# Output projection of both layers: token tiles taken in pairs, seven half-size products for eight

## The reference, cut to what matters

```
for layer in range(DEPTH):                     # DEPTH = 2
    h = rms_norm(x, norm_g[layer])
    cols = split_columns(h @ w_in[layer])
    ... y_gdn, y_mla, y_rwkv
    mix = jnp.concatenate([y_gdn, y_mla, y_rwkv], axis=-1)
    mix = mix * jax.nn.silu(cols['gate'])
    x = x + mix @ w_out[layer]                 # (1024 x 1024) @ (1024 x 1024), float32
return rms_norm(x, final_norm_g)               # then the second block
```

## Time and profile before

| | us |
|---|---|
| median of 3 runs | 3735.61 (3733.98 to 3739.67) |
| span of the profiled execution | 3728.9 |
| stage `out0`, first transpose to last VectorE write | 1028.55 to 1160.73 |
| stage `out1`, the same | 2153.04 to 2301.77 |
| TensorE busy in the span | 3471.1 (93%) |
| VectorE busy | 2265.8 (61%) |
| ScalarE busy | 1230.6 (33%) |

### The profile page before, as it was taken

The page is one execution under the profiler, slowest core; times in us unless marked ns, Lnnn a source line. Parts: engine busy times, 40 slices in busy tenths (PEclk is TensorE's granted clock), DMA queues, the critical chain, the costliest instruction groups (busy, mean ns, idle before and its releaser), DMA issues. The chain is left out here.

```text
span 3728.9 us, 65858 instructions
## 1 busy us (share of the span) xinstructions
PE 3471.1 (93%) x27928; PEld 2115.2 (57%) x27928; DVE 2265.8 (61%) x4019; ACT 1230.6 (33%) x2149; POOL 285.3 (8%) x233
## 2 busy tenths in 40 slices
PE   7888989989999889988999988999999997999999
PEld 4367446666644467445676644666666664444444
DVE  3586468876653477458976653567766667433453
ACT  3353354535432254354534532122212221321002
POOL 0010100000000011100000000222222220000000
PEclk9999999999999999999999999999999998999999
DMA  4334112220053333312220042111111102213221
GB/s 164 105 92 129 63 40 85 81 101 12 10 190 117 98 93 100 95 40 85 79 104 12 9 157 82 35 45 42 46 41 46 41 23 89 87 41 112 90 96 45
DMA packets 302164, 281.51 MB, mean 75 GB/s; under 512 B 18208, under 2 KB 274592, under 8 KB 301872
## 3 DMA queue, kind: packets, MB, share of 16 engines
q1 hardware_dynamic: 301872, 277.30, 23.1%
HBM read 203.93 MB, written 73.33 MB: 74 GB/s over the span
## 5 line engine op out<-in xcount | busy, mean ns | idle before, releaser
L3528 DVE SCALAR_TENSOR_TENSOR cv<-glu,params,cv 128x1024 f32<-128x1024 f32 x240 | 361.0, 1504 | 6.4
L1542 PE MATMUL ps<-hT,w_cols 128*128 128x512 f32 x576 | 254.6, 601 | 8.3 <-PEq L160 8.3
L413 PE MATMUL ps<-hT,w_cols 128*128 128x512 f32 x448 | 196.0, 595 | 1.6 <-PEq L160 1.6
L1542 PEld LDWEIGHTS ps<-hT,w_cols 128*128 128x128 f32 x576 | 110.8, 193 | 147.2 <-issue 145.3
L3824 PE MATMUL ps<-hT,wr 128*128 128x512 f32 x360 | 161.7, 592 | 0.0
L413 PEld LDWEIGHTS ps<-hT,w_cols 128*128 128x128 f32 x448 | 84.1, 190 | 109.3 <-issue 109.3
L3504 POOL TENSOR_TENSOR Sp<-Sp,Rp 128x520 f32<-128x520 f32 (+1 forms) x56 | 88.5, 1581 | 564.2 <-DVE W L3545 564.2
L3287 PE MATMUL ps<-hT,w_f 128*128 128x347 f32 x384 | 116.1, 462 | 5.4 <-DMA w_f<-in_w_in 5.4
L3302 PE MATMUL ps<-w_i,hT 128*128 128x128 f32 x1024 | 120.7, 277 | 0.0
L3302 PEld LDWEIGHTS ps<-w_i,hT 128*128 128x128 f32 x1024 | 116.1, 192 | 2.2 <-issue 1.6
L3824 PEld LDWEIGHTS ps<-hT,wr 128*128 128x128 f32 x360 | 68.4, 190 | 86.1 <-issue 86.1
(11 more groups left out here) (936 smaller groups left out, 7137.6 us busy)
## 6 DMA issues: line engine op xcount, KB each, us to landing
w_cols<-in_w_in SPq DMA_DIRECT2D x32, 512.0 KB, 3.9
wr<-in_w_in SPq DMA_DIRECT2D x24, 512.0 KB, 5.2
hT_hbm<-hT SPq DMA_DIRECT2D x2, 4096.0 KB, 14.1
hT<-hT_hbm SPq DMA_DIRECT2D x2, 4096.0 KB, 16.1
fh<-hT_hbm SPq DMA_DIRECT2D x16, 512.0 KB, 4.6
fh_again<-hT_hbm SPq DMA_DIRECT2D x16, 512.0 KB, 4.6
x<-in_x SPq DMA_DIRECT2D x8, 512.0 KB, 9.3
ahead<-kb_hbm SPq DMA_DIRECT2D x16, 256.0 KB, 3.4
```

The costliest lines, as they stand in the source:

```text
L413: q = pe.matmul(ps[:, proj_bank(n, b), :], lhsT=wc[:, n % 3, k, :], rhs=hT[:, k, P + b * 512:P + (b + 1) * 512], start=(k == 0), stop=(k = ...
L1542: q = pe.matmul(ps[:, proj_bank(n, b), :], lhsT=wc[:, n % 3, k, :], rhs=hT[:, k, P + b * 512:P + (b + 1) * 512], start=(k == 0), stop=(k = ...
L3528: vec.scalar_tensor_tensor(out=cv[:, h % 2, :], in0=src, scalar=w, in1=cv[:, h % 2, :], op0=ALU.mult, op1=ALU.add).then_inc(*VEC(f"tap{h}_ ...
```

## The change

Token tiles are multiplied in four pairs. A pair's left operand (two tiles, 256 x 1024) and the weights (1024 x 1024) are each cut into 2x2 blocks; seven products of blocks (each four matmuls of 128x512: P1 to P7) replace eight. VectorE makes four combinations of the weights once per layer (`combos_open`, `combos_close`: T1 to T4, 128x2048 each) and four of the left operand per pair (`sums_of_left`, `last_sum`: S1 to S4, 128x512 each). Three products go on adding to one chain bank, and ScalarE copies the bank's intermediate values out in between (`keep(1..3, p)`). VectorE adds for three of a pair's four output blocks a kept value and a bank (`block_of`), for the fourth the chain bank. The combinations lie in a new buffer (layer 0) or in one that is free (layer 1), and in `hT` where it is not yet written. The odd tile of a pair is finished first; the even tile waits for P3, which TensorE does after P1 of the next pair. `mixed` is split in `moments(p)` and `mixed(p)`. `residual(p)` now waits for `normed{2p-4}`, the later of the pair's two.

The core of the diff (the index-only edits of SP's stores and the helpers for views are left out):

```
@@ sync
                         def residual(p):
                             if p >= 2:
                                 sp.wait_ge(*DMA[f"x_out{p - 2}"])
-                                sp.wait_ge(*VEC[f"normed{2 * p - 3}"])
+                                sp.wait_ge(*VEC[f"normed{2 * p - 4}"])
...
                         branches(2)
+                        store(1)
                         store(0)
-                        store(1)
                         residual(2)
                         branches(3)
@@ scalar
+                        def keep(n, p):
+                            act.wait_ge(*PE[f"{('P1', 'P6', 'P7')[n - 1]}_{p}"])
+                            if p:
+                                act.wait_ge(*VEC[f"y{('11', '12', '22')[n - 1]}_{p - 1}"])
+                            act.copy(kept[:, n - 1, :], ps[:, chain_bank(p), :]).then_inc(*ACT(f"s{n}_{p}"))
...
                         silu(1)
-                        scales(1)
-                        silu(2)
+                        keep(1, 0)
+                        keep(2, 0)
                         if LAST:
                             meta_norm()
+                        scales(1)
+                        keep(3, 0)
+                        silu(2)
                         turned(2)
-                        norms(0)
-                        scales(2)
                         turned(3)
...
+                        for p in range(1, NP):
+                            keep(1, p)
+                            norms(2 * p - 1)
+                            if p + 1 < NP:
+                                scales(p + 1)
+                            keep(2, p)
+                            norms(2 * p - 2)
+                            keep(3, p)
+                            if p + 2 < NP:
+                                silu(p + 2)
+                            if p + 1 < NP:
+                                turned(2 * p + 2)
+                                turned(2 * p + 3)
@@ vector
+                        combos_open()
+                        sums_of_left(0)
+                        combos_close()
+                        last_sum(0)
+                        moments(1)
+                        block_of(0, 0, 0)
                         mixed(1)
...
+                        block_of(0, 1, 1)
+                        block_of(0, 1, 0)
+                        for p in range(1, NP):
+                            sums_of_left(p)
+                            if LAST and p == 1:
+                                hidden("_m", -1)
+                            ended(2 * p - 1)
+                            if p + 1 < NP:
+                                moments(p + 1)
+                            normed(2 * p - 1)
+                            block_of(p - 1, 0, 1)
+                            last_sum(p)
+                            hidden(f"{2 * p - 1}", 2 * p - 1)
+                            ended(2 * p - 2)
+                            if p + 1 < NP:
+                                mixed(p + 1)
+                            normed(2 * p - 2)
+                            block_of(p, 0, 0)
+                            hidden(f"{2 * p - 2}", 2 * p - 2)
+                            block_of(p, 1, 1)
+                            block_of(p, 1, 0)
@@ tensor
+                        def product(name, p, to, a, b, start=True):
+                            for k in range(4):
+                                q = pe.matmul(ps[:, to, :].rearrange("p (a n) -> p a n", a=2), lhsT=a[:, k, :], rhs=b[:, k], start=(start and k == 0), stop=(k == 3),
+                                              skip_group_check=True)
+                            q.then_inc(*PE(f"{name}_{p}"))
...
+                        def sixth(p):
+                            pe.wait_ge(*VEC[f"S2_{p}"])
+                            if p == 0:
+                                pe.wait_ge(*VEC["T2"])
+                            pe.wait_ge(*ACT[f"s1_{p}"])
+                            product("P6", p, chain_bank(p), sm[:, 1], D2, start=False)
...
+                        first(0)
+                        second(0)
+                        sixth(0)
+                        fifth(0)
+                        seventh(0)
+                        turn(2)
+                        turn(3)
+                        fourth(0)
...
+                        for p in range(1, NP):
+                            first(p)
+                            third(p - 1)
+                            sixth(p)
+                            second(p)
+                            hidden_tile(2 * p - 1)
+                            seventh(p)
+                            fifth(p)
+                            if p + 1 < NP:
+                                turn(2 * p + 2)
+                            hidden_tile(2 * p - 2)
+                            fourth(p)
+                            if p + 1 < NP:
+                                turn(2 * p + 3)
+                        third(NP - 1)
```

More of the change, by code:

```diff
@@ L3041, in mixed, with combos_open @@
                             vec.tensor_tensor(m, m, gate[p % 2][:, :, :], ALU.mult).then_inc(*VEC(f"mix{p}"))
[L3043 to L3048, removed]
+                        def combos_open():
+                            vec.tensor_tensor(D1, right(0, 1), right(0, 0), ALU.subtract).then_inc(*VEC("T1"))
+                            vec.wait_ge(*VEC["T1"])
+                            vec.tensor_tensor(D2, right(1, 1), D1, ALU.subtract).then_inc(*VEC("T2"))
@@ L3087, in _ @@
                             vec.tensor_scalar(xn[:, 1, :], xm[:, :], m_rs[:, :], None, ALU.mult).then_inc(*VEC("normed_m"))
[L3088 to L3106, removed]
+                        block_of(0, 1, 1)
[19 more added lines that the diff above has]
+                            block_of(p, 1, 0)
+                        ended(NT - 1)
+                        block_of(NP - 1, 0, 1)
+                        normed(NT - 1)
+                        ended(NT - 2)
+                        hidden(f"{NT - 1}", NT - 1)
+                        normed(NT - 2)
                         hidden(f"{NT - 2}", NT - 2)
-                        hidden(f"{NT - 1}", NT - 1)
                     @block.tensor
@@ L3130, in hidden_tile @@
                         def hidden_tile(t):
[L3131 removed]
+                            before = t + 1 if t % 2 == 0 else t - 3
+                            hidden(f"{t}", xn[:, t % 2], before if before >= 0 else "_m" if LAST else None)
+                        def product(name, p, to, a, b, start=True):
[3 more added lines that the diff above has]
+                            q.then_inc(*PE(f"{name}_{p}"))
@@ new lines, in first, with second @@
+                        def first(p):
+                            pe.wait_ge(*ACT[f"mT{2 * p}_0"])
+                            if p >= 2:
+                                pe.wait_ge(*VEC[f"x{2 * (p - 2) + 1}"])
+                            product("P1", p, chain_bank(p), left(p, 0, 0), right(0, 0))
+                        def second(p):
+                            pe.wait_ge(*ACT[f"mT{2 * p}_1"])
+                            if p:
+                                pe.wait_ge(*VEC[f"c11_{p - 1}"])
+                            product("P2", p, B_BANK, left(p, 0, 1), right(1, 0))
@@ new lines, in third @@
+                        def third(p):
+                            pe.wait_ge(*VEC[f"S4_{p}"])
+                            pe.wait_ge(*VEC[f"c22_{p}"])
+                            product("P3", p, D_BANK, left(p, 0, 1), right(1, 1), start=False)
+                        def sixth(p):
[4 more added lines that the diff above has]
+                            product("P6", p, chain_bank(p), sm[:, 1], D2, start=False)
@@ new lines, in seventh, with fifth @@
+                        def seventh(p):
+                            pe.wait_ge(*VEC[f"S3_{p}"])
+                            if p == 0:
+                                pe.wait_ge(*VEC["T3"])
+                            pe.wait_ge(*ACT[f"s2_{p}"])
+                            product("P7", p, chain_bank(p), left(p, 1, 0), right(0, 1), start=False)
+                        def fifth(p):
+                            if p:
+                                pe.wait_ge(*VEC[f"x{2 * p - 2}"])
+                            product("P5", p, D_BANK, sm[:, 0], D1)
@@ L3133, in _, with fourth @@
+                        def fourth(p):
+                            if p == 0:
+                                pe.wait_ge(*VEC["T4"])
+                            pe.wait_ge(*ACT[f"s3_{p}"])
+                            product("P4", p, chain_bank(p), left(p, 1, 1), D4, start=False)
                         turn(0)
                         turn(1)
[L3135 to L3149, removed]
```

97 lines of the change are left out of this document (71 added, 26 removed).

## The result

| | median us | runs | ratio to before, 95% interval |
|---|---|---|---|
| before | 3734.80 | 4 | |
| change | 3758.31 (3755.26 to 3765.72) | 4 | 1.006 (1.0047 to 1.0073) |
| change, a second time | 3756.64 (3754.72 to 3757.89) | 4 | 1.006 (1.0047 to 1.0074) |

The account below looks back on a forecast made before the run. TensorE, busy 93% of the span, was taken as the bound. Added waits and low clock, less 13.7 us saved per layer, gave +12 and +10 us, +22 in all: median 3758 us (+0.6%), own range 3749 to 3769.

Parts of the forecast that it names:

- the queueing at the stage's start: First pair of each stage: TensorE waits 1.3, 4.0, 4.6 plus 2.15 clock in layer 0; 3.3, 5.35, 2.05, 2.15 in layer 1.
- the early gate: Rival at tile 5: pair 3's gate lands early enough for tile 4's copies; 3731 us, or 3719; chance 0.11.
- the odd tile's wait: Layer 1, pairs 1 and 2: the odd tile's `normed` stands behind table load, root, final and `moments`: 2.3 us.

## What to carry to other kernels

When a pairing or an algebraic saving reorders the finish of tiles, follow each "buffer free" wait in the DMA queue and everything queued behind it: here one wait for a tile that now ends later held an unrelated transfer of the next pair, an activation in front of the copies waited for that transfer, and this chain alone cost 26 to 28 us, as much as the products saved. With the queueing at the stage's start a saving of 27 us became a loss of 23. Requests whose buffers are free belong ahead of requests that must wait, and in an engine's program order a copy that TensorE needs belongs ahead of an operation that waits for DMA. Walking the chain with durations of the old trace gave both the loss and the time with the early gate within a few microseconds, before anything ran.

## What the runs showed of the hardware

- Filling a wait of TensorE with unneeded products made the kernel faster: 48 added matmul instructions in two places, 8 us less, of which about 4 are traced to the clock staying at 1.00 right behind them.
- Waits of 2 us had no fixed price. In `out1`, behind the odd tile's wait, the product took 5.37 us in the second profile of the change and 4.40 in the first, where the transposes ahead of it were slow as well (1.97 us); after another wait of 2.06 and 2.05 us it took 3.67 in both. A sum should take such losses as a range.
- The silu of pair 1 waits for its gate, which is asked for at the same point of the same queue. It started 11.4 us after the stage's first transpose in the first profile of the change and 9.9 in the second, as in the profile of before. One profiled execution fixes such a landing only to about 1.5 us.
